# Second mixture-of-experts layer: experts sorted on the chip by token count, 28 steps of 128 rows and 18 shared steps of two times 64 rows, weights used as float32

## What is computed

```python
scores = jax.nn.sigmoid(xf @ w_router)                       # 512 x 64
# each token keeps TOP_K = 6 of 64 experts, gate = its 6 scores, scaled to sum to 2.5
xb = x_pad[tok]                                              # the rows of one expert
hb = jax.nn.silu(xb @ w_exp_gate[e]) * (xb @ w_exp_up[e])    # 1024 -> 256
y  = (hb @ w_exp_down[e]) * g[:, None]                       # 256 -> 1024
routed = segment_sum(y, tok)                                 # 512 x 1024
out = shared + routed                                        # shared: a dense expert, all rows
```

## Time and profile before

| | us |
|---|---|
| device time, median of 3 runs | 1964.89 |
| profiled execution, first to last instruction (span) | 1960.0 |
| median less span | 4.9 |
| PE busy | 1791.1 (91%) |
| DVE busy | 1007.4 (51%) |
| ACT busy | 781.5 (40%) |
| POOL busy | 560.3 (29%) |
| first gate and up product of the second experts | 1239.9 |
| last copy of a result of the second experts | 1924.3 |

### The profile page before, as it was taken

One profiled execution on the slowest core, in us unless ns is written; L12 is line 12 of the kernel. 1 busy time (PEld: TensorE's weight loads), 2 busy tenths in 40 slices (PEclk: granted clock), 3 DMA queues, 4 the chain that ended last, 5 costly groups with the idle time before them and its releaser, 6 DMA issues. The chain is left out here.

```text
span 1960.0 us, 24773 instructions
## 1 busy us (share of the span) xinstructions
PE 1791.1 (91%) x7962; PEld 1151.2 (59%) x7962; DVE 1007.4 (51%) x1976; ACT 781.5 (40%) x1404; POOL 560.3 (29%) x435
## 2 busy tenths in 40 slices
PE   6989999989999959999999699899999999999992
PEld 3434446754333337776788575677666766666661
DVE  1866416431111036632633354777767777677673
ACT  2412217311111135633632122566655655565551
POOL 4997807011111118801100000222222322222221
PEclk9789999989999979999999899999999999999996
DMA  5353410668999853222022444599999999999873
GB/s 193 129 182 108 172 43 5 247 253 335 406 406 403 340 165 130 87 87 92 1 86 101 162 184 155 206 342 339 337 327 321 337 333 339 328 325 328 324 249 108
DMA packets 116829, 441.71 MB, mean 225 GB/s; under 512 B 27428, under 2 KB 31924, under 8 KB 79368
## 3 DMA queue, kind: packets, MB, share of 16 engines
q1 hardware_dynamic: 93672, 406.94, 55.1%
q0 software_dynamic: 23040, 33.64, 7.4%
q10 hardware_dynamic: 32, 0.04, 0.0%
HBM read 438.34 MB, written 55.11 MB: 252 GB/s over the span
## 5 line engine op out<-in xcount | busy, mean ns | idle before, releaser
L1885 DVE TENSOR_TENSOR big_parts<-big,h_cols_parts 128x1024 fp32r<-128x1024 f32 x256 | 305.7, 1221 | 48.0 <-ACT h_cols_parts L1938 41.0
L2149 POOL DMA_INDIRECT acc_scratch<-heads,small x80 | 131.4, 1642 | 530.3 <-DVE small L1916 303.8
L1938 ACT ACTIVATE h_cols_parts<-big 128x1024 fp32r<-128x1024 f32 x256 | 262.7, 1060 | 27.7 <-PE bank L1844 24.5
L1875 PE MATMUL bank<-big,heads 128*128 128x512 f32 x512 | 236.1, 604 | 0.8 <-ACT heads L1946 0.8
L1842 PE MATMUL bank<-h_cols_parts,heads_parts 128*128 128x512 f32 x512 | 205.5, 401 | 2.2 <-DVE heads_parts L1905 2.2
L1844 PE MATMUL bank<-h_cols_parts,heads_parts 128*128 128x512 f32 x512 | 200.2, 391 | 0.0
L1843 PE MATMUL bank<-big_parts,heads_parts 128*128 128x512 f32 x512 | 199.3, 389 | 0.0
L1875 PEld LDWEIGHTS bank<-big,heads 128*128 128x128 f32 x512 | 92.5, 190 | 93.3 <-issue 92.3
L458 PE MATMUL bank<-big,h_cols 128*128 128x512 f32 x320 | 144.7, 607 | 0.3 <-ACT heads L608 0.3
L1971 ACT ACTIVATE heads<-bank 128x512 f32<-128x512 f32 x64 | 38.3, 599 | 237.8 <-DMA acc_scratch<-heads,small 201.8
L1842 PEld LDWEIGHTS bank<-h_cols_parts,heads_parts 128*128 128x128 f32 x512 | 96.7, 189 | 20.2 <-DVE heads_parts L1905 2.5
(11 more groups left out here) (430 smaller groups left out, 3353.3 us busy)
## 6 DMA issues: line engine op xcount, KB each, us to landing
big<-in_w_exp_gate_dram SPq DMA_DIRECT2D x86, 1024.0 KB, 17.6
big<-in_w_exp_up_dram SPq DMA_DIRECT2D x86, 1024.0 KB, 25.7
big<-in_w_exp_down_dram SPq DMA_DIRECT2D x72, 1024.0 KB, 18.2
big<-in_w_in_dram SPq DMA_DIRECT2D x13, 2048.0 KB, 8.8
junk_and_spare<-in_w_mod_dram SPq DMA_DIRECT2D x24, 1024.0 KB, 5.3
x_res<-in_w_exp_down_dram SPq DMA_DIRECT2D x16, 1024.0 KB, 18.1
big<-in_w_out_dram SPq DMA_DIRECT2D x4, 2048.0 KB, 9.0
h_rows<-in_w_exp_down_dram SPq DMA_DIRECT2D x8, 1024.0 KB, 21.0
```

The source lines that it names most:

```text
L1875: mm = pe.matmul(b_y[half][:, :], hidt[:, b, P * j:P * j + P], dn[q][:, j, 512 * half:512 * half + 512], start=j == 0, stop=j == FH - 1)
L1885: dve.tensor_tensor(gu_low[q][:, :, part, :], gu[q][:, :, part, :], gu_high[:, :, part, :].bitcast(F32), ALU.subtract).then_inc(w_low, 1)
L1938: act.activation(gu_high[:, :, part, :], gu[q][:, :, part, :], ACT.Copy).then_inc(w_high, 1)
L2149: return pool.indirect_dma_start(out=K.acc_dram, out_offset=bass.IndirectOffsetOnAxis(at, 0), in_=rows, in_offset=None, bounds_check=S - 1 ...
```

## The change

Four things are done together.

**1. The experts are sorted on the chip** (`ExpertOrder`). From the counts DVE makes a key for each expert. Experts 0 to 3 get fixed places 0 to 3 so that their weights can be loaded before the counts are known; the other 60 are sorted by count. The comparison of each key with each other is summed over experts by a product, and the one-hot table of places gives the expert numbers (`ids`, for SP) and permutes the tables of ranks and gates. PE does four small products for it between the units of the shared expert's down product. SP reads each expert's number from `ids` by a register load before it issues its weights.

**2. 46 steps instead of 64** (`expert_steps`). Places 0 to 3 and the 24 heaviest others take steps of 128 rows. The 36 lightest share 18 steps of two times 64 rows. The order is 4 fixed steps and then six times full, shared, full, shared, full, shared, full. Ranks of light experts are counted from 65 on, so that a light expert with over 64 rows would pass 128 and set off the overflow stage.

**3. Float32 products.** The gate and up product is no longer split: 8 products instead of 24 for a full step, 16 half-width ones for a shared step. The work of ACT and DVE that made the parts is gone. The memory that it frees gives six gate and up buffers and four down buffers.

**4. Second half of the accumulator.** In a shared step one token can stand in both experts' rows. The second expert's rows go to rows 512 to 1023 of `acc2_dram`. These are zeroed during the second attention, read back after the last shared step, and added to x by DVE at the end of the stage.

The heart of the diff, in this order: the steps, PE's gate and up product, POOL's waits ahead of the first gather, SP's loads, DVE after its last step, and the shared expert's stores, where `between` waits for `ids` and loads the gate and up weights of places 4 and 5:

```diff
+STATIC, FULL, SHARED = 4, 24, 18
+def expert_steps():
+    full = [(STATIC + n,) for n in range(FULL)]
+    first = STATIC + FULL
+    shared = [(first + 2 * n, first + 2 * n + 1) for n in range(SHARED)]
+    steps = [(n,) for n in range(STATIC)]
+    for n in range(6):
+        a, b = full[4 * n:4 * n + 4], shared[3 * n:3 * n + 3]
+        steps += [a[0], b[0], a[1], b[1], a[2], b[2], a[3]]
...
+            for i in steps:
...
+                    for c in range(KC):
+                        if len(places) == 1:
+                            mm = pe.matmul(b_au[b][:, :], xt[:, b, P * c:P * c + P], gu[places[0][0]][:, :, c, :], start=c == 0,
+                                           stop=c == KC - 1)
+                        else:
+                            for n, part in enumerate(rows):
+                                mm = pe.matmul(b_au[b][part, :], xt[:, b, P * c + HALF * n:P * c + HALF * n + HALF],
+                                               gu[places[n][0]][:, :, c, :], start=c == 0, stop=c == KC - 1)
...
-                            pe.matmul(b_au[b][:, :], x_high, gu_high[:, :, c, :], start=c == 0, stop=False)
-                            pe.matmul(b_au[b][:, :], x_high, gu_low[q][:, :, c, :], start=False, stop=False)
-                            mm = pe.matmul(b_au[b][:, :], x_low, gu_high[:, :, c, :], start=False, stop=c == KC - 1)
...
+            pool.wait_ge(K.acc_stored, 16 * T)
+            pool.wait_ge(K.acc2_lower, 16 * T)
...
+            for n in range(4, total):
+                if n + 2 < total:
+                    sp.wait_ge(au_mm, weights.step_of[n - 4] + 1)
+                    weights.gate_up(sp, n + 2)
+                sp.wait_ge(y_mm, weights.step_of[n - 4] + 1)
+                weights.down(sp, n)
+            sp.wait_ge(scattered, 16 * (last_shared + 1))
+            for t in range(T):
+                sp.dma_start(lower[:, t, :], K.acc2_dram[S + P * t:S + P * t + P, :]).then_inc(K.acc2_lower, 16)
...
+            dve.wait_ge(K.acc2_lower, 32 * T)
+            for t in range(T):
+                step(dve.tensor_tensor(lower[:, t, :], lower[:, t, :], K.gain[:, :], ALU.mult))
+                step(dve.tensor_tensor(K.x[:, t, :], K.x[:, t, :], lower[:, t, :], ALU.add))
...
     def sync(sp, between):
         for t in range(T):
             sp.wait_ge(y_taken, 2 * t + 2)
-            sp.dma_start(K.acc_dram[P * t:P * t + P, :], K.hr[:, t, :]).then_inc(stored, 16)
+            sp.dma_start(K.acc2_dram[P * t:P * t + P, :], K.hr[:, t, :]).then_inc(stored, 16)
+            if t == 1:
+                between(sp)
```

More of the change, by code:

```diff
@@ L1259, in _ @@
             if shared:
-                shared.down(pe)
+                shared.down(pe, order.products)
             else:
@@ L1332, in _ @@
                                    float(NO_TOKEN), None, ALU.add))
+            if order:
+                order.constants(dve, step)
+                dve.wait_ge(K.products, at_rank[0])
+                order.vector(dve, step)
+                return
             step(dve.tensor_copy(m.parts[:, :, :, 2], m.gate))
@@ L1379, in _ @@
                 preload.above_job_slots(sp)
-                shared.sync(sp)
+                shared.sync(sp, order.loads)
 def first_output(K):
@@ L1413, in first_downs @@
+    steps = expert_steps()
+    slots = [slot for step in steps for slot in step]
+    step_of = [i for i, step in enumerate(steps) for _ in step]
     def first_downs(self, sp):
-        for e in range(3):
-            self.down(sp, e, e)
+        self.gate_up(sp, 0)
+        self.down(sp, 0)
     def above_job_slots(self, sp):
-        self.gate_up(sp, 2, 2)
+        self.down(sp, 1)
     def into_job_slot(self, sp, n):
-        self.gate_up(sp, n, n)
+        self.gate_up(sp, 1 + n)
+        if n == 1:
+            self.gate_up(sp, 3)
@@ new lines, in sorted_experts_stage, with gate_up_places @@
+    y_mm, y_dve, y_act = s("moe2_down_product"), s("moe2_y_dve_copied"), s("moe2_y_act_copied")
+    row_dmas = s("moe2_row_dmas")
+    lower = K.big[:, 8192:12288].rearrange("p (t d) -> p t d", t=T)
+    last_shared = max(i for i, step in enumerate(steps_of) if len(step) == 2)
+    first_n = [weights.step_of.index(i) for i in range(N)]
+    steps = range(-4, N + 1)
+    has = lambda i, d: 0 <= i + d < N
+    def gate_up_places(i):
+        return [(n % weights.GATE_UP, 32 * (n // weights.GATE_UP + 1))
+                for n in range(first_n[i], first_n[i] + len(steps_of[i]))]
@@ L1821, in experts_stage, with down_places @@
+    def down_places(i):
+        return [(n % weights.DOWN, 16 * (n // weights.DOWN + 1)) for n in range(first_n[i], first_n[i] + len(steps_of[i]))]
     with nc.Block(no_gpsimd_drain=True) as block:
@@ L1932, in _ @@
         @block.scalar
         def _(act):
-            def high(i, r, k):
-                q, part = (r + 1) % 3, slice(two * k, two * k + two)
-                if late(i, 0):
-                    act.wait_ge(*((w_used, (PARTS - 1) * i + (k + 1)) if k < PARTS - 1 else (au_mm, i + 1)))
-                act.activation(gu_high[:, :, part, :], gu[q][:, :, part, :], ACT.Copy).then_inc(w_high, 1)
-            def step(i, r, has, fills):
-                if has(-1):
-                    b = (r - 1) % 2
+            for i in steps:
+                if has(i, -1):
+                    b = (i - 1) % 2
@@ L1974, in _ @@
         @block.gpsimd
         def _(pool):
-            pool.memset(f[:, 0:2048], 0.0).then_inc(cleared, 1)
-            pool.wait_ge(cleared, 1)
-            for ready, n in init:
-                pool.wait_ge(ready, n)
-            def step(i, r, has, fills):
-                if has(3):
-                    b, q = (r + 3) % 2, (r + 3) % 6
-                    pool.wait_ge(idx_ready, 2 * i + 8)
-                    if late(i, -1):
+            step = K.pool.on(pool)
+            step(pool.memset(f[:, 0:2048], 0.0))
@@ L1986, in step @@
+            pool.wait_ge(K.rows_stored, 16 * T)
+            pool.wait_ge(K.acc_stored, 16 * T)
+            pool.wait_ge(K.acc2_lower, 16 * T)
+            for i in steps:
+                if has(i, 3):
+                    b, q = (i + 3) % 2, (i + 3) % 6
+                    pool.wait_ge(idx_ready, 3 * i + 12)
+                    if i >= -1:
                         pool.wait_ge(xt_mm, 2 * i + 4)
@@ L2952, in turn, with down @@
             at_ht.append(product(K, mm))
-    def down(pe):
+    def down(pe, between):
         w = w_down
@@ L2965, in down @@
             at_y.append(product(K, mm))
+            between(pe, u)
     def scalar(act):
```

423 lines of the change are left out of this document (250 added, 173 removed).

## The result

| | before | after |
|---|---|---|
| device time, median of 4 runs each, us | 1964.06 | 1919.13 |
| lowest to highest | 1961.93 to 1966.2 | 1914.47 to 1922.9 |
| ratio after/before, 95% interval | | 0.9768 (0.9752 to 0.9784) |
| profiled execution, span, us | 1960.0 | 1919.8 |

The change makes the kernel 44.9 us faster. 107 us were predicted (1858 us, range 1834 to 1892), so the sign was right and the size was not. The profiled execution after took 1921.6 us, 1.8 more than its span.

What follows compares the result with a forecast made beforehand. Before, PE bound light experts and scatters heavy ones; afterwards weights would. The 1960.0 us span, +8 at the start, -121.5 in the second experts, +7 at the end, gave 1853.5, with 4.9 of offset 1858 us, range 1834 to 1892.

Steps and rivals of the forecast that it cites:

- What bounds: Second experts: before, PE paces light experts and scatters heavy ones; after the change, the weights become the bound.
- The DMA term and the stall: Second experts: 35.4 MB per group of seven steps take 88 us against PE's 82.5, giving 22 us of stall.
- signs of being wrong: In the stage: PE idle with DMA under 380 GB/s, copies released by scatters each step, or a clock under 1.00 mid-stage.
- What a wait costs: Second experts: 22 us of stall added at its own length; a lower clock counted only at the stage's start, 1 us.
- PE's own time: Second experts: 28 full steps of 11.5 us and 18 shared of 12.15 us, 541 us to the last copy.
- Weights late all the way: Rival, 24%: once the lead is gone, second experts take 9.0 us each, stage 590 to 606, total 1885 to 1901 us.
- PE alone: Rival, 10%: buffers and lead cover the second experts' weights at 424 GB/s; stage 541 us, total 1834 us.
- Scatters set the pace: Rival, 3%: scatter time grows with rows, 46 second-expert steps at 14.8 us, 681 us, no gain, about 1975 us.
- The Trainium skill's figure: Second experts: an HBM limit of about 358 GB/s would make a group 99 us, the stage some 75 us longer.
- Start: Start of the second experts: first gather 6 us late behind weight loads, plus small products; +8 us, bounds +3 and +12.
- End: Last copy to last block: reading back 2 MB and eight DVE operations add +7 us, bounds +3 and +10.
- The offset of 4.9: Whole kernel: the three runs' median stands 4.9 us above the profiled span, added to 1853.5 for 1858 us.

Runs made afterwards that it cites:

- e3: Changed kernel without loading the up weights after the first six experts, a third of the weights' bytes; 1854.73 us, 0.9442 of the kernel before.
- e10: Changed kernel with the second experts' gather row numbers outside the table, so only scatters move rows; 1882.09 us, 0.9573 of the kernel before.
- e9: Changed kernel with the second experts' scatter row numbers outside the table, so only gathers move rows; 1852.31 us, 0.9423 of the kernel before.
- e8: Changed kernel with the second experts' gather and scatter row numbers outside their tables, so no rows move; 1852.93 us, 0.9431 of the kernel before.
- e2: Changed kernel with two filler products ahead of each shared step's down product, to keep the clock; 1926.67 us, 0.9813 of the kernel before.
- e7: Changed kernel with every expert alone, 64 steps of 128 rows, keeping sorting, float32 products and buffers; 2048.07 us, 1.043 of the kernel before.
- e1: Changed kernel with the loads of places 4 and 5 behind all four stores of the shared rows; 1913.70 us, 0.9746 of the kernel before.
- e11: Changed kernel with place 4 and 5 loads behind all four stores, and 44 reordered steps, two full ones last; 1901.21 us, 0.9674 of the kernel before.

## Why the prediction was wrong, point by point

**What bounds: right.** Weights are the bound once steps are shared, PE's waits are for them (e3) and stand at shared steps, from the 13th iteration on, and neither ACT's and DVE's lost work nor the register loads show.

**The DMA term and the stall: the step that failed.** The prediction gave the rows "1.5 times" the part that they have in the first experts, "so 6%, and 89 us a group", and took 88. The bytes were right, but a group took 92 by the experiments' full rates: 31.5 MB at 407 GB/s are 77.4 us without rows, 33.5 at 409 with gathers 82.0, 33.5 at 387 with scatters 86.6, 35.4 at 384 with both 92.1. So gathers add 4.6 us, the price of their bytes, and scatters 9.2, twice that. The prediction's own arithmetic with this number and PE's measured 83.5 us a group (82.5 was taken) comes near the waits: (92.1 - 83.5) x 6 = 52, less the lead of 11 is 41, and 43 were measured. The agreement is rough. With 0.99 as the limit of the full rate a group is 91 us and the same sum 33; and for e10, (86.6 - 83.5) x 6 = 19, and 19 were measured, so the lead hardly helped there. In e9 a group's 82.0 is under PE's 83.5, and no wait is left.

The profile of before had the price in two lines that the prediction did not use: SP's queue moved 406.94 MB in 55.1% of the span, 377 GB/s of its engine time, POOL's 33.64 MB in 7.4%, 232 GB/s. A group by these is 31.5 MB at the 406 of the first experts and 4.0 at 232, 77.6 + 17.2 = 95 us, a little too much; at the bytes' price alone it was 88.

I had two causes in one factor, read off 424 against 406 GB/s. Doubling the adds alone would not have mended it: the first experts' rate without rows would be 406 x (6.3 + 0.26 x 3) / (6.3 + 0.52) = 421 GB/s, and 37.4 MB at 421 are 89 us, where the prediction already stood. The rest is the ground rate: 407 GB/s here, or 415 with the limit at 0.99, and not 421. Why it is lower in this stage was not settled; the 424 of the earlier trace rows is a mean over 12 us only. So the price of the adds is shown, and what made 92 of 88 is in good part this open rest.

Two of the prediction's own signs of being wrong were there: PE idle at 370 GB/s, under its 380, and a clock of 0.96 in the stage. It read the first as "buffers or SP's order"; e8 to e10 show that the rows' traffic did it.

**What a wait costs: missed.** The stall was counted at its own length. After each of the six waits of 3.9 to 4.3 us PE ran on at the lower clock (1.06 us a record and not 0.59, at a granted clock of 0.50), which cost 1.4 to 3 us a time; so it did after some of the waits of 1.2 to 2.6 us and not after others. e8 and e9 have no wait, and their stages are 550.7 (1259.85 to 1810.57) and 550.4 us (1257.66 to 1808.03). After's 615.4 is 550.5 + 43 of waits + 22, and the 22 is the clock: by the granted clock the stage loses 24 us, e9's 2. The prediction mentions the clock at the start of the stage and puts it at nothing in the stage, where it took half as much as the waits. This is an account of PE's time. That the stage would be 22 us shorter at full clock is not shown; e2, the one try, brought half of the clock back and was slower.

**PE's own time: 550.5 and not 541.** e7's iterations are 11.60 us, the predicted 11.55. In the mixed order a full iteration is 11.86 and a shared one 11.94 to 12.10, 0.2 us more for a pair of them than forecast; with the first iteration at half clock and shared lists this is 9.5 us. The stage's excess is then 9.5 + (43 - 22) + 22 = 52.5, the 52.4 of the table.

**The rivals.** "Weights late all the way" (24%) named what happened, with waits from the 13th iteration to the last, and its 1885 to 1901 was also too low, since it too counted rows by their bytes and no clock. "PE alone" fell. "Scatters set the pace" fell in its own sense: in the stage POOL waited 20.6 us for scatters (7 times) and ACT 14.0 (4 times), but PE for none, so that cost nothing, as forecast. But scatters did set the pace in another way, as traffic. No overflow stage ran.

**The Trainium skill's figure.** The prediction weighed about 358 GB/s (the Trainium skill, "DMA: Bandwidth & Descriptors", Specifications) and a group of 99 us; its 75 us for the stage were a little high, since 11 us in six groups are 66. The measured 92 lies between 99 and my 88. The 384 to 409 GB/s of after and e8 to e10, like the 406 of the first experts, speak against 358 as a limit for this core. The Trainium skill, "Perfetto Trace Analysis", Roofline, has the note that the figure is a core's share with its neighbour active, and that a core alone can go above it, to about 435. The rates here agree with that.

**Start: +12.8 and not +8**, a little above its upper bound of 12. The mechanism was right in part: the first gather went out 9.6 us late and not 6, and e1, which undoes the order, gives back 4.1 us in the profile and 5.4 in the median. The gather itself then took 3.0 us longer than before, with the weights' transfers beside it, where 1 was taken. The eight turned rows at half clock cost the 1 us that was taken for the clock. The first product at half clock (8.9 us and not 7.0) falls behind this cut and is part of the stage's 550.5, since e8 and e9 have it too.

**End: +9.9 and not +7**, inside its bounds of 3 to 10: the read took 9.8 us from its issue to DVE's start, with the last scatter beside it, where 7 was taken. e11 takes all of it back.

**Before the stage: +6.8, no part of the prediction.** 3.9 us of it arise near 400 to 480 us, in code that the change leaves alone, ahead of the zeroing. PE's router products there (L1221) in the profile of after and of e1:

```profile
402.80 3.58 PE L1221 MATMUL bank<-small,h_cols 128*128 128x36 f32 x16 [0.73 <-ACT h_cols L1277]
```

```profile
403.34 1.97 PE L1221 MATMUL bank<-small,h_cols 128*128 128x36 f32 x16 [0.73 <-ACT h_cols L1277]
```

The two programs are the same up to there; one execution had the full clock and the other half, and so it is in six and six of the twelve profiles with the change. At the row of ACT that stands at 958.17 before (L1088; L1089 after the change) the twelve are between 3.3 us sooner (e1) and 6.6 later (e8) than before, and after itself is 4.9 later; nearly all the code up to there is unchanged, so this spread is the execution. But from there to the down product, which starts at 1213.29 to 1222.14, each of the twelve loses another 1.8 to 3.1 us against the one profile of before. That much seems to be the change's; by what is open.

**The offset of 4.9.** It was the median of three runs less one execution's span, and mixed two things. For the profiled execution after, time less span is 1.8.

## What to carry to other kernels

Price DMA traffic by engine time and not by bytes: here a row scattered with an add cost the queues 1.9 times what a gathered or a plainly stored one did, and the share column against the MB of each queue's line shows it before any experiment. Where PE will wait for a few us at a time, count what the clock takes after the waits, here half as much again. And when a change merges work so that transfers become the bound, fewer instructions on PE give back little (24 us gave 8): look for bytes, adds, and what stands first in the queue.

## What was not expected of the hardware

- Adding scatters: 12.56 MB in 60.9 us of the 16 engines, gathers 12.57 MB in 31.4, plain stores at the gathers' rate. The costs are not a sum: gathers alone +0, scatters alone +30, both +66 us, since PE's 83.5 us a group is a threshold that 82.0 doesn't pass, 86.6 passes a little and 92.1 far.
- A wait of 3.96 us was followed by some 5 us at a granted clock of 0.50, with the DMA engines at 392 GB/s in the same window.
- The clock in short, thin products differs from one execution of the same code to the next (3.58 or 1.97 us for the same 16 products), and executions of the same code stand up to 10 us apart at 958 us.
